# Two f32 halves for the second output piece of each group turn, and a later place for two low halves and six taps in VectorE's turn

## The chip, the cores and the metric
One core of a Trainium2 chip runs the whole program. The metric is the device time of the program in microseconds (us). There is no other core and no collective.

## The reference, cut to what matters
The reference is two model blocks in float32 on 256 tokens of width 1024. The first block computes `proj = rms_norm(x) @ w_in`. One part of it goes through a gated 31-tap depthwise convolution and a layer norm (the convolution branch), one through a grouped state-space branch of 8 groups, and the rest becomes gates. What the change touches is the end of the state-space branch:

```
y = ssd_chunked(...)                       # 8 groups, 256 channels each
y = y * silu(z)
yg = y.reshape(bsz, seqlen, N_GROUPS, D_INNER // N_GROUPS)
yg = yg * rsqrt(mean(yg * yg, axis=-1) + RMS_EPS)
y = yg.reshape(...) * norm_g
return y @ out_w                           # 2048 x 1024
```

Then come `w_out`, a feed-forward part, and a second block with its own projections. All of these are products of 256 tokens with large weight matrices that are read from HBM once.

## The kernel before, in words
All weights come as one stream of pieces, each 128 x 1024 f32 (512 KB), through a ring of 8 slots `raw`. SyncE starts the load of piece p when slot p % 8 is free, strictly in order of p (L415 to L427). Activations lie transposed, with channels on the 128 partitions and the 256 tokens on the free axis.

A piece is multiplied in one of two ways. In the usual way ScalarE copies it into `w_hi`, rounded to the TensorE format fp32r (L965), VectorE forms `w_lo` = `raw` - `w_hi` (L1457, "the low half"), and TensorE runs three matmuls for each 128 x 128 tile: hi x lo, hi x hi, lo x hi (`tile`, L485 to L490). The operand has such halves as well. In the native way a piece of the set `NATIVE` is multiplied in plain f32 straight from `raw` (L731 for the output pieces); the profile has two matmul records for each such matmul. Pieces of the set `LOW` get their low half in a third way: ScalarE writes minus `w_hi` into `w_lo` (L974), and a DMA issued by GpSimd adds `raw` to it (L462). The slot of a native piece is free when TensorE has used it, that of a usual piece when its low half is made, that of a `LOW` piece when its DMA has landed.

The eight groups run as a software pipeline. Group 0 has its own first turn. A hardware loop runs the turns of groups 1 to 6, and group 7 has a last turn with another mix of work (`more=False` in VectorE's `group_turn`). A turn of the loop takes eight pieces: six input pieces, at offsets 0, 1, 3, 4, 5, 7, and two output pieces of the group before, at offsets 2 and 6, both native. Between the pieces TensorE does small steps of the group: `cb` (L693), `x_transposes` (L701), `y_products` (L710), `y_transposes` in the middle of the second output piece (L718), and at the end `y_scale` (L611), which needs the scale that GpSimd forms from the group norm's mean square ("the moment").

The order of work on each engine is written out by hand. The names that matter:

- TensorE: `group_turn` at L738, `out_piece` at L725. The last turn follows the loop at L753 to L766. It goes on with input pieces of the gates, and at L762 to L766 it waits for `conv_sum_ready`, the sum over channels of the convolution, to compute its mean (L765).
- ScalarE: `group_turn` at L1099. It makes the high halves six pieces ahead, `silu_bc` (L1061) and `silu_x` (L1066) once VectorE has made the short convolution, `decays` (the exponential at L1081), the squares of y with their row sums (L1087), and drains of the input pieces from PSUM. The last turn stands at L1162 to L1189.
- VectorE: `group_turn` at L1724. The short convolution `conv_inputs` (L1658, twelve instructions), the taps of the 31-tap convolution (L1493, or `late_taps`, L1720, in the last turn), `masked_scores` (L1671, waits for `cb`), `x_by_dt` (L1676), `decayed_scores` (L1683, waits for `decays`, and TensorE's `y_products` waits for it), `y_gated` (L1692, L1696), the moment `y_mean` (L1467), `y_normed` (L1709), and between them one low half at each call of `lo()`. In the last turn the low halves and late taps are followed by six more taps (L1813), one low half (L1815), the channel sum (L1823), and the memset that signals `conv_sum_ready` (L1827).

Low halves in VectorE's loop turn, by offset from the turn's first piece: 8 after the short convolution, 11 after `y_gated`, 13 before `y_normed`. Offsets 7, 9 and 12 are `LOW`, so their call of `lo()` does nothing. In the last turn none but 1 and 4 is `LOW`, and VectorE makes 7 and 8 before `masked_scores`, 9 and 10 before the moment, 11, 12, 13 and 14 behind it.

Of the kernel before, what the change touches and what calls it, by code (L numbers as in the profile page):

```python
# [21 lines left out]
P = 128  # L22
# [53 lines left out]
DOWN2 = UP2 + 2 * KF2  # L76
PIECES = DOWN2 + KF2
GLU_NATIVE = (0, 1, 2, 3, 9)
NATIVE = frozenset(GLU_NATIVE) | frozenset([LOOP0 + 8 * i + n for i in range(GROUPS - 1) for n in OUT_AT]) | frozenset(range(TAIL0, PW0))
# [51 lines left out]

def split_order(p, turn=0):

    return sum(q not in NATIVE and q not in LOW for q in range(p)) + 1 + (6 - len(LOW_AT) if p < GATES0 else 8) * turn


def low_turn(p):
# [29 lines left out]
def hybrid_kernel(nc, x_in, weights, params_in, w_dt, lru_w, consts, out):  # L167
    cs_dram = nc.dram_tensor("cs_dram", [HEADS + HPG, T], F32).ap()
    stack = ExitStack()
    with stack:  # L170
# [22 lines left out]
        s0a = ExitStack()  # L193
        m_stage = sb("m_stage", [P, 2 * T], F32R, s0a)
        s0a.close()
        stage = sb("stage", [P, 2, T])
        stage2 = sb("stage2", [P, 2, T])
        sp = sb("sp", [P, 8, KD])
# [163 lines left out]
        cb_ready, cb_used, xt_ready, xdt_ready = sem("cb_ready"), sem("cb_used"), sem("xt_ready"), sem("xdt_ready")  # L362
        dec_ready, m_ready, y_ready, yz_ready = sem("dec_ready"), sem("m_ready"), sem("y_ready"), sem("yz_ready")
        yt_ready, first_tap = sem("yt_ready"), sem("first_tap")
        conv_operand_ready, mixed_ready = sem("conv_operand_ready"), sem("mixed_ready")
        m_copied = sem("m_copied")
        conv_high, conv_low = sem("conv_high"), sem("conv_low")
# [114 lines left out]
        def _(pe):  # L482
# [239 lines left out]
            def y_scale(g):  # L722
                spread_scale(g + 2)

            def out_piece(p, turn, g, c, between=None):  # L725
                native_loaded(p, turn)
                pe.wait_ge(scale_read, g + 2)
                for m in range(KD):
                    if between is not None and m == KD // 2:
                        y_transposes(between)  # L730
                    ins = mm(acc_out(m), raw[:, p % RING, m * P:(m + 1) * P], yn[:, c, :], start=False, stop=False,  # L731
                             skip_group_check=True)
                ins.then_inc(pieces_done, 1)
# [217 lines left out]
        def _(act):  # L951
# [131 lines left out]
            def y_squares(g):  # L1083
# [3 lines left out]
                    ins = F(ysq[:, t, :], A[3][:, t * T:(t + 1) * T], ACT.Square, accum_out=ysum[:, t:t + 1])  # L1087
                ins.then_inc(sums_ready, 1)

            for s in range(6):  # L1090
                split_hi(SSM0 + s + LEAD)
                drain_input(s, s, SSM0 + s, 0)
                if s == 2:
                    act.wait_ge(scale_read, 1)
                    exponents(0)
                if s == 3:
                    first_taps(0)

            def group_turn(g, base, t):  # L1099

                def split(n):
                    split_hi(base + n + LEAD, t)

                split(1)
                split(2)
                silu_bc(g)
                drain_input(0, 0, base + IN_AT[0], t)
                split(3)
                drain_input(1, 1, base + IN_AT[1], t)
# [50 lines left out]


            g = GROUPS - 1  # L1162
            for n in range(3):
                split_hi(GATES0 + n + LEAD)
            silu_bc(g)

            def conv_operand(c):

# [275 lines left out]
        def _(dve):  # L1444
# [256 lines left out]
            def y_normed(g, read=None):  # L1701
# [9 lines left out]
                        own.up(ins)  # L1711
                ins.then_inc(scale_read, 1)

            def late_taps(cs, ks=LATE_TAPS):

                last = {c: own.value() for c in cs}
                for k in ks:
                    for c in cs:
                        after(last[c])
                        last[c] = own.up(V.scalar_tensor_tensor(acc[:, c, :], v[:, c, k:k + T],  # L1720
                                                                col("conv_dw_w", c * CONV_K + k), acc[:, c, :],
                                                                ALU.mult, ALU.add))

            def group_turn(g, los, read=None, turn=0, more=True, first=True):  # L1724
# [7 lines left out]

                if first:
                    conv_inputs(g, (0, 1))
                    lo()
                    conv_inputs(g, (2, 3))
                lo()
                looped = more and first
                if looped:
                    taps(g + 1, LONG_TAPS[:2], start="sum")  # L1740
                masked_scores(g)
                turn_taps = LONG_TAPS[2:] if looped else LOOP_TAPS
                if not first:
                    lo()
                    more_taps(0, LOOP_TAPS[12:])
                    add_parts(0)
                    after(own.value())
                if looped:
                    more_taps(g + 1, turn_taps[:6])
                elif more:  # L1750
                    taps(g + 1, turn_taps[:6], start="sum")
                else:
                    late_taps((0, 1))
                x_by_dt(g)
                decayed_scores(g)
                lo()
                if more:
                    more_taps(g + 1, turn_taps[6:12])
                else:
                    late_taps((2, 3))  # L1760
                y_gated(g)
                lo(1 if first else 2)
                if more:
                    more_taps(g + 1, turn_taps[12:18])
                else:
                    late_taps((4, 5))
                if looped:
                    lo()
                    y_mean(g)
                else:  # L1770
                    y_mean(g)
                    lo()
                if more:
                    more_taps(g + 1, turn_taps[18:])
                    add_parts(g + 1)
                else:
# [620 lines left out]
```

## Time and profile before

| what | value |
|---|---|
| device time, median of 3 | 906.33 us (906.28 to 906.91) |
| the profiled execution | 907.11 us, span 905.0 us |
| TensorE (PE) busy | 895.5 us, 99% |
| VectorE (DVE) busy | 745.6 us, 82% |
| ScalarE (ACT) busy | 589.9 us, 65% |
| GpSimd (POOL) busy | 38.0 us, 4% |
| granted TensorE clock | 0.999 |

The difference of 2.1 us between the profiled execution's time and its span lies outside the instructions. Matmuls are pipelined: a matmul record of 0.28 us starts 0.12 us behind the one before it, so distances between starts are the cost, and not durations. The same holds in small for VectorE and ScalarE, where the next instruction often starts 0.1 us before the end that is shown.

### The profile page before, as it was taken

The page shows a single profiled execution, that of the slowest core. Times are in us where ns is not written, and L with a number is a line of the kernel's source. Part 1 is how long each engine was busy: PE and PEld are TensorE (multiplying, and loading weights), DVE is VectorE, ACT ScalarE, POOL GpSimd, SP SyncE. Part 2 cuts the span into 40 slices and gives each one's busy share as a digit, 9 for nine tenths or more (in the row PEclk, how much of TensorE's full clock was granted, in tenths as well). Part 3 has the DMA queues.
Part 4 walks back from the last instruction along what each step waited for, and adds up shares of the span by engine and source line. Part 5 has one row for each costly group of instructions (what it writes and reads, how often), then busy time and mean ns, then how long its engine had stood idle before and what let it go on. Part 6 is the DMA issues. An engine that isn't in the chain of part 4 may idle for free.

```text
span 905.0 us, 18388 instructions
## 1 busy us (share of the span) xinstructions
PE 895.5 (99%) x6629; PEld 846.7 (94%) x6629; DVE 745.6 (82%) x1387; ACT 589.9 (65%) x1020; POOL 38.0 (4%) x50
## 2 busy tenths in 40 slices
PE   9999999999999999999999999999999999999997
PEld 7999999999999999998888889989999999999886
DVE  5999898889889988889988666889979988888543
ACT  5649878798777485666666636679656756666432
POOL 1000111111110000000000000100000000000000
PEclk9999999999999999999999999999999999999999
DMA  8576578878876647447655555355447465555601
GB/s 335 179 270 228 146 196 237 243 209 242 227 202 207 210 146 251 163 141 248 204 186 185 197 187 171 123 194 188 144 137 258 148 202 183 178 180 177 232 2 46
DMA packets 48511, 172.05 MB, mean 190 GB/s; under 512 B 5668, under 2 KB 6344, under 8 KB 48328
## 3 DMA queue, kind: packets, MB, share of 16 engines
q1 hardware_dynamic: 43488, 154.74, 51.2%
q0 software_dynamic: 2880, 10.49, 6.1%
q10 hardware_dynamic: 2088, 6.08, 1.8%
q8 instruction: 35, 0.57, 0.2%
q14 instruction: 20, 0.16, 0.1%
HBM read 159.72 MB, written 1.09 MB: 178 GB/s over the span
## 4 chain that ended last, share of the span: by engine, by line
PE 68%; issue 24%; DVE 6%; ACT 1%; DMA 1%; POOL 1%; SPq 0%; POOLq 0%; DVEq 0%
PE A L488 10%; PE A L489 10%; PE A L490 10%; PE B L731 6%; PE A L522 4%; PE B L522 3%; PE B L812 2%; PE B L488 2%; PE B L489 2%; PE B L490 2%; PE A L524 2%; DVE w_lo L1457 2%; PE B L524 2%; PE A L812 2%; PE A L501 1%
## 5 line engine op out<-in xcount | busy, mean ns | idle before, releaser
L1457 DVE TENSOR_TENSOR w_lo<-raw,w_hi 128x1024 fp32r<-128x1024 f32 x249 | 301.8, 1220 | 63.5 <-ACT w_hi L965 62.4
L965 ACT ACTIVATE w_hi<-raw 128x1024 fp32r<-128x1024 f32 x249 | 259.2, 1051 | 69.9 <-PE A L813 20.6
L488 PE MATMUL A<-h,w_hi 128*128 128x256 f32 x957 | 276.0, 288 | 0.2 <-DVE sc L2120 0.2
L490 PE MATMUL A<-h,w_lo 128*128 128x256 f32 x957 | 270.7, 283 | 0.0
L489 PE MATMUL A<-h,w_hi 128*128 128x256 f32 x957 | 270.6, 283 | 0.0
L488 PEld LDWEIGHTS A<-h,w_hi 128*128 128x128 f32 x957 | 183.4, 192 | 3.3 <-issue 2.6
L489 PEld LDWEIGHTS A<-h,w_hi 128*128 128x128 f32 x957 | 183.5, 192 | 0.3
L490 PEld LDWEIGHTS A<-h,w_lo 128*128 128x128 f32 x957 | 183.3, 192 | 0.0
L488 PE MATMUL B<-h,w_hi 128*128 128x256 f32 x352 | 100.1, 284 | 0.0
L489 PE MATMUL B<-h,w_hi 128*128 128x256 f32 x352 | 99.6, 283 | 0.0
L490 PE MATMUL B<-h,w_lo 128*128 128x256 f32 x352 | 99.6, 283 | 0.0
L1493 DVE SCALAR_TENSOR_TENSOR part<-v,par,part 128x256 f32<-128x256 f32 x178 | 73.6, 479 | 0.0
L488 PEld LDWEIGHTS B<-h,w_hi 128*128 128x128 f32 x352 | 67.5, 192 | 0.8 <-issue 0.8
L489 PEld LDWEIGHTS B<-h,w_hi 128*128 128x128 f32 x352 | 67.5, 192 | 0.0
L490 PEld LDWEIGHTS B<-h,w_lo 128*128 128x128 f32 x352 | 67.5, 192 | 0.0
L812 PE MATMUL B<-hid,w_hi 128*128 128x512 f32 x184 | 64.1, 392 | 0.0
L731 PE MATMUL B<-yn,raw 128*128 128x256 f32 x256 | 59.1, 379 | 0.0
L522 PE MATMUL A<-h,w_hi 128*128 128x512 f32 x160 | 56.8, 399 | 0.0
L731 PEld LDWEIGHTS B<-yn,raw 128*128 128x128 f32 x256 | 47.0, 190 | 5.5
L813 PE MATMUL B<-hid,w_lo 128*128 128x256 f32 x184 | 51.4, 280 | 0.0
L812 PE MATMUL A<-hid,w_hi 128*128 128x512 f32 x138 | 48.1, 392 | 0.0
L522 PE MATMUL B<-h,w_hi 128*128 128x512 f32 x128 | 45.4, 399 | 0.0
(345 smaller groups left out, 1655.9 us busy)
## 6 DMA issues: line engine op xcount, KB each, us to landing
raw<-in_weights_dram SPq DMA_DIRECT2D x289, 512.0 KB, 4.4
w_lo<-raw POOLq DMA_DIRECT2D x20, 512.0 KB, 4.8
csrow<-cs_dram ACTq DMA_DIRECT2D x9, 512.0 KB, 4.8
x<-in_x_dram SPq DMA_DIRECT2D x4, 256.0 KB, 4.5
bd<-in_lru_w_dram ACTq DMA_DIRECT2D x1, 1024.0 KB, 5.5
out_dram<-m_wide SPq DMA_DIRECT2D x3, 256.0 KB, 2.1
raw<-in_weights_dram SPq DMA_DIRECT2D x2, 256.0 KB, 4.9
par<-in_params_dram SPq DMA_DIRECT2D x1, 379.0 KB, 6.6
```

What stands on the lines that cost most here:

```text
L488: mm(dst, wh, lo, start=first, stop=False, skip_group_check=free)
L489: mm(dst, wh, hi, start=False, stop=False, skip_group_check=free)
L490: return mm(dst, wl, hi, start=False, stop=last, skip_group_check=free)
L501: ins = mm(dst, raw[:, p % RING, k * P:(k + 1) * P], operand[:, k, :], start=k == 0, stop=k == KD - 1)
L522: mm(bank, w_hi[:, p % RING, k * P:(k + 1) * P], h[:, k, :], start=k == 0, stop=False, skip_group_check=True)
L524: ins = mm(bank[:, 0:T], w_lo[:, p % RING, k * P:(k + 1) * P], h_hi[:, k, :], start=False, stop=k == KD - 1, skip_group_check=True)
L731: ins = mm(acc_out(m), raw[:, p % RING, m * P:(m + 1) * P], yn[:, c, :], start=False, stop=False, skip_group_check=True)
L812: mm(DOWN_BANKS[m], wh, hid[:, k, :], start=first, stop=False, skip_group_check=True)
L813: return mm(DOWN_BANKS[m][:, 0:T], w_lo[:, slot, j * P:(j + 1) * P], hid_hi[:, k, :], start=False, stop=last, skip_group_check=True)
L965: F(w_hi[:, s, :], raw[:, s, :], ACT.Copy).then_inc(hi_ready, 1)
L1457: V.tensor_tensor(w_lo[:, s, :], raw[:, s, :], w_hi[:, s, :].bitcast(F32), ALU.subtract).then_inc(lo_ready, 1)
L1493: ins = V.scalar_tensor_tensor(dst, vs(k), w(k), dst, ALU.mult, ALU.add)
```

## The change: what it does
The second output piece of each turn (offset 6), for seven turns, leaves the set `NATIVE`. It is multiplied with `tile`, from `w_hi` and `w_lo`, with halves of the operand `yn` for its channel block: ScalarE makes `yn_hi` (`y_high`), VectorE `yn_lo` (`y_low`), in two new tiles. ScalarE's `split(0)` at the turn's start makes the piece's high half, and VectorE its low half. The slot of the piece is then free at its low half instead of at the end of its product.

In VectorE's loop turn the low halves are now 6 and 8 before the moment and 11 and 13 behind it (13 behind `y_normed`), and the taps 2 + 12 before it and 10 behind (before: 2 + 18 and 4). In the last turn it makes 6, 7 and 8 between `decayed_scores` and the moment, 9 and 10 right behind the moment, and 11, 12 and 13 behind `y_normed`. ScalarE's last turn gets the high half of piece 6 ahead of `silu_bc`, and those of 7 and 8 and `y_high` behind it.

```
-NATIVE = ... | frozenset([LOOP0 + 8 * i + n for i in range(GROUPS - 1) for n in OUT_AT]) | ...
+NATIVE = ... | frozenset([LOOP0 + 8 * i + OUT_AT[0] for i in range(GROUPS - 1)]) | ...
-    return ... + (6 - len(LOW_AT) if p < GATES0 else 8) * turn
+    return ... + (7 - len(LOW_AT) if p < GATES0 else 8) * turn
...
             def out_piece(p, turn, g, c, between=None):
-                native_loaded(p, turn)
-                pe.wait_ge(scale_read, g + 2)
+                split = p not in NATIVE
+                if split:
+                    split_ready(p, turn)
+                    pe.wait_ge(yn_low, g + 1)
+                else:
+                    native_loaded(p, turn)
+                    pe.wait_ge(scale_read, g + 2)
...
+                    if split:
+                        ins = tile(p % RING, m, yn_hi[:, c, :], yn_lo[:, c, :], acc_out(m), False, False, True)
+                        continue
...
+            def y_high(g, cs=(1,)):
+                act.wait_ge(scale_read, g + 2)
+                for c in cs:
+                    ins = F(yn_hi[:, c, :], yn[:, c, :], ACT.Copy)
+                ins.then_inc(yn_high, 1)
...
+                split(0)
                 split(1)
                 split(2)
                 silu_bc(g)
+                y_high(g - 1)
...
-            for n in range(3):
-                split_hi(GATES0 + n + LEAD)
+            split_hi(GATES0 + LEAD)
             silu_bc(g)
+            split_hi(GATES0 + 1 + LEAD)
+            y_high(g - 1)
+            split_hi(GATES0 + 2 + LEAD)
...
+            def y_low(g, cs=(1,)):
+                dve.wait_ge(yn_high, g + 1)
+                for c in cs:
+                    ins = V.tensor_tensor(yn_lo[:, c, :], yn[:, c, :], yn_hi[:, c, :].bitcast(F32), ALU.subtract)
+                ins.then_inc(yn_low, 1)
...
                 if first:
                     conv_inputs(g, (0, 1))
+                    conv_inputs(g, (2, 3))
+                else:
                     lo()
-                    conv_inputs(g, (2, 3))
-                lo()
...
+                cut = (4, 8, 12) if looped else (6, 12, 18)
...
                 decayed_scores(g)
                 lo()
+                if first:
+                    y_low(g - 1)
                 if more:
-                    more_taps(g + 1, turn_taps[6:12])
+                    more_taps(g + 1, turn_taps[cut[0]:cut[1]])
...
                 y_gated(g)
-                lo(1 if first else 2)
+                lo(2)
...
-                if looped:
-                    lo()
-                    y_mean(g)
-                else:
-                    y_mean(g)
-                    lo()
+                y_mean(g)
+                lo(2 if first else 1)
                 if more:
-                    more_taps(g + 1, turn_taps[18:])
+                    more_taps(g + 1, turn_taps[cut[2]:])
                     add_parts(g + 1)
                 else:
                     late_taps((6, 7))
-                lo()
+                if not first:
+                    lo()
                 y_normed(g, read)
                 lo(len(los))
```

## Rows read from the trace of the kernel before

**Rows 1.** The page: busy time, share of the span and instructions of each engine.
```profile
PE 895.5 (99%) x6629; PEld 846.7 (94%) x6629; DVE 745.6 (82%) x1387; ACT 589.9 (65%) x1020; POOL 38.0 (4%) x50
```

**Rows 2.** Waits of PE, 85 to 345 us: who waited for whom, in total, times, longest.
```profile
PE A L611 <- POOL scale L450: 0.5, 1, 0.5
```

**Rows 3.** Timeline of PE, turn of 134.41 us: start, length, engine, line, what.
```profile
147.22 0.60 PE L701 MATMUL A<-cst,gb 128*128 128x128 f32 x4
147.58 0.36 PE L488 MATMUL A<-h,w_hi 128*128 128x256 f32 x1
147.78 0.28 PE L489 MATMUL A<-h,w_hi 128*128 128x256 f32 x1
...
154.99 0.28 PE L490 MATMUL A<-h,w_lo 128*128 128x256 f32 x1
155.11 1.89 PE L731 MATMUL B<-yn,raw 128*128 128x256 f32 x8
...
158.82 0.47 PE L488 MATMUL A<-h,w_hi 128*128 128x256 f32 x1
159.12 0.28 PE L489 MATMUL A<-h,w_hi 128*128 128x256 f32 x1
```

**Rows 4.** Timeline of DVE in loop turns: convolution, a low half and what follows.
```profile
163.33 4.84 DVE L1658 SCALAR_TENSOR_TENSOR gb<-ubuf,par,gb 128x256 f32<-128x256 f32 x12
...
182.19 1.22 DVE L1457 TENSOR_TENSOR w_lo<-raw,w_hi 128x1024 fp32r<-128x1024 f32 x1
183.33 2.46 DVE L1493 SCALAR_TENSOR_TENSOR part<-v,par,part 128x256 f32<-128x256 f32 x6
...
204.08 1.76 DVE L1683 TENSOR_TENSOR dec<-dec,cbm 128x1536 f32<-128x1536 f32 x1
```

**Rows 5.** Timeline of ACT in loop turns: squares, exponential, a copy behind its load.
```profile
130.91 0.36 ACT L1087 ACTIVATE ysq<-A 128x256 f32<-128x256 f32 x1
...
147.29 1.49 ACT L1081 ACTIVATE dec<-dec 128x1536 f32<-128x1536 f32 x1
...
181.46 1.06 ACT L972 ACTIVATE w_hi<-raw 128x1024 fp32r<-128x1024 f32 x1 [2.39 <-DMA raw<-in_weights_dram]
...
212.74 0.38 ACT L1087 ACTIVATE ysq<-A 128x256 f32<-128x256 f32 x1
```

**Rows 6.** Timeline of PE: turn starts (L488), and the y products (L710).
```profile
189.60 0.36 PE L488 MATMUL A<-h,w_hi 128*128 128x256 f32 x1
...
205.90 0.66 PE L710 MATMUL A<-dec,xdt 128*64 128x256 f32 x4
...
217.27 0.36 PE L488 MATMUL A<-h,w_hi 128*128 128x256 f32 x1
...
272.46 0.36 PE L488 MATMUL A<-h,w_hi 128*128 128x256 f32 x1
```

**Rows 7.** The chain that ended last, in the last turn: start, length, what.
```profile
282.60 0.56 DVE cbm L1671
...
298.92 1.60 POOL scale L450
```

**Rows 8.** Timeline of DVE in the last turn and behind it.
```profile
277.65 1.23 DVE L1457 TENSOR_TENSOR w_lo<-raw,w_hi 128x1024 fp32r<-128x1024 f32 x1 [1.10 <-ACT w_hi L965]
...
311.91 0.27 DVE L1827 MEMSET part<- 128x256 f32 x1 [0.19 <-DVE sq_sum L1823]
```

**Rows 9.** Timeline of PE: the matmuls that wait for the memset's signal.
```profile
312.35 1.08 PE L765 MATMUL A<-sq_sum,cst 128*128 128x256 f32 x4
```

**Rows 10.** Timeline of ACT in the last turn: from L1061 to the exponential.
```profile
278.46 0.71 ACT L1061 ACTIVATE gb<-gb 128x256 f32<-128x256 f32 x2
...
283.01 1.49 ACT L1081 ACTIVATE dec<-dec 128x1536 f32<-128x1536 f32 x1
```

**Rows 11.** Timelines of ACT and DVE: a high and a low half of 256 tokens.
```profile
328.12 0.42 ACT L1172 ACTIVATE conv_hi<-acc 128x256 fp32r<-128x256 f32 x1
...
328.57 0.43 DVE L1845 TENSOR_TENSOR conv_lo<-acc,conv_hi 128x256 fp32r<-128x256 f32 x1
```

More of the change, by code:

```diff
@@ L78 @@
 GLU_NATIVE = (0, 1, 2, 3, 9)
-NATIVE = frozenset(GLU_NATIVE) | frozenset([LOOP0 + 8 * i + n for i in range(GROUPS - 1) for n in OUT_AT]) | frozenset(range(TAIL0, PW0))
+NATIVE = frozenset(GLU_NATIVE) | frozenset([LOOP0 + 8 * i + OUT_AT[0] for i in range(GROUPS - 1)]) | frozenset(range(TAIL0, PW0))
 LOW_AT = (1, 4, 7)
@@ L132, in split_order @@
 def split_order(p, turn=0):
-    return sum(q not in NATIVE and q not in LOW for q in range(p)) + 1 + (6 - len(LOW_AT) if p < GATES0 else 8) * turn
+    return sum(q not in NATIVE and q not in LOW for q in range(p)) + 1 + (7 - len(LOW_AT) if p < GATES0 else 8) * turn
 def low_turn(p):
@@ L195, in hybrid_kernel @@
         s0a.close()
+        s0 = ExitStack()
+        yn_hi = sb("yn_hi", [P, 2, T], F32R, s0)
+        yn_lo = sb("yn_lo", [P, 2, T], F32R, s0)
+        s0.close()
         stage = sb("stage", [P, 2, T])
@@ L364, in hybrid_kernel @@
         yt_ready, first_tap = sem("yt_ready"), sem("first_tap")
+        yn_high, yn_low = sem("yn_high"), sem("yn_low")
         conv_operand_ready, mixed_ready = sem("conv_operand_ready"), sem("mixed_ready")
@@ L723, in y_scale, with split_ready @@
                 spread_scale(g + 2)
-            def out_piece(p, turn, g, c, between=None):
-                native_loaded(p, turn)
-                pe.wait_ge(scale_read, g + 2)
+            def split_ready(p, turn):
+                if p in LOW:
+                    pe.wait_ge(low_added[(p - LOOP0) % RING], 16 * low_turn(p) + 16 * turn)
+                else:
+                    pe.wait_ge(lo_ready, split_order(p, turn))
+            def out_piece(p, turn, g, c, between=None):
+                split = p not in NATIVE
[5 more added lines that the diff above has]
+                    pe.wait_ge(scale_read, g + 2)
                 for m in range(KD):
@@ L1734, in group_turn @@
                     conv_inputs(g, (0, 1))
-                    lo()
-                    conv_inputs(g, (2, 3))
-                lo()
+                    conv_inputs(g, (2, 3))
+                else:
+                    lo()
                 looped = more and first
@@ L1748, in group_turn @@
                 if looped:
-                    more_taps(g + 1, turn_taps[:6])
+                    more_taps(g + 1, turn_taps[:cut[0]])
                 elif more:
@@ L1761, in group_turn @@
                 y_gated(g)
-                lo(1 if first else 2)
+                lo(2)
                 if more:
-                    more_taps(g + 1, turn_taps[12:18])
+                    more_taps(g + 1, turn_taps[cut[1]:cut[2]])
                 else:
                     late_taps((4, 5))
-                if looped:
-                    lo()
-                    y_mean(g)
-                else:
-                    y_mean(g)
-                    lo()
+                y_mean(g)
+                lo(2 if first else 1)
                 if more:
-                    more_taps(g + 1, turn_taps[18:])
+                    more_taps(g + 1, turn_taps[cut[2]:])
                     add_parts(g + 1)
```

## The prediction
> **What bounds the kernel now.** I read the page first, then who TensorE waits for in the stretch of the group turns, then its timeline there, then the same turns on VectorE and ScalarE, and last the chain that ended last. TensorE is busy 99%, VectorE 82%, ScalarE 65% [rows 1]. Between 85 and 345 us TensorE waits once, 0.5 us, for the scale of the last turn [rows 2]. So in the six loop turns (27.6 us each: 189.60 to 217.27 is 27.67 [rows 6]) it is the bound and every tenth taken from it would count, provided that nobody else comes late.
>
> Two places are nearly late already. The first is inside the loop turn: `y_products` starts 1.82 us behind the start of `decayed_scores` in the turn of 189.60 (204.08 [rows 4], 205.90 [rows 6]), because it waits for it. That is 16.30 us into the turn, where the other turns have 16.21; so the slack there is nothing. The second is the last turn. There the chain that ended last leaves TensorE at 282.60 and runs on VectorE to the moment and GpSimd at 298.92 [rows 7]. Behind it the memset that signals `conv_sum_ready` starts at 311.91 [rows 8] and the matmul that waits for it at 312.35 [rows 9], 0.44 us later, with no gap that shows as a wait. VectorE thus sets TensorE's time, or all but sets it, from 282.6 to 312.
>
> **TensorE's saving.** A usual tile's three matmuls start 0.12 us apart (154.99 to 155.11). Now the second output piece with the transposes in it takes from 155.11 to the next piece's second matmul at 159.12, 4.01 us. With halves it is 24 starts of 0.12 us, plus the transposes: 0.36 us from 147.22 to 147.58, then 0.20 instead of 0.12 us to 147.78, and 0.12 us to the next piece's second matmul: 2.87 + 0.36 + 0.08 + 0.12 = 3.43 us [rows 3]. That is -0.58 us a turn, -4.06 us for seven, if everything is in time. About 0.30 of the 0.58 lies in the piece's first half, ahead of the transposes.
>
> The trace prices the native piece at 3.71 us less its transposes, and the same piece in halves at 2.87. The Trainium skill (FP8 and Floating Point Precision, TensorE Precision Notes) has true f32 take four passes through the array. Against three passes that would be 4/3 of 2.87, or 3.83 us, and a saving of nearly 1 us a piece instead of 0.58; it would be 6.7 us in all, an estimate from that page's pass count. The rows decide, and they say less.
>
> **VectorE's and ScalarE's added work.** A turn gains one high half on ScalarE (1.06 us long [rows 5], 0.95 as a distance) and `y_high` (0.42, distance about 0.32 [rows 11]), and on VectorE one low half (182.19 to 183.33, 1.14 us [rows 4]) and `y_low` (0.43, distance 0.34 [rows 11]). As sums these fit. VectorE at 82% has some 3 us idle in a turn of 27.6, and needs 1.5. No DMA is added; the piece's slot comes free at its low half, some 17 us into the turn instead of 24.4, so loads start earlier if at all. The wait of `out_piece` for `yn_low` is met about 3 us ahead, and `yn_low` itself waits for `y_high`, ready 8 us ahead.
>
> **Where it doesn't fit: the ring through the loop.** Follow ScalarE around. From the squares of y (130.91) to the next turn's exponential (147.29) it is busy nearly without a gap: 16.38 us; the exponential is 1.49 us long [rows 5]. Then `decayed_scores` to `y_products` is 1.82 us, and from `y_products` to the squares of the same turn 205.90 to 212.74 is 6.84 us [rows 5, 6]. Around: 16.38 + 1.53 + 1.82 + 6.84 = 26.57 us, under the turn's 27.6. The change puts the high half and `y_high` ahead of the exponential, +1.27, and takes 0.30 from the last leg: 27.54 us. That is above the 27.02 that TensorE alone would need. So the turn takes about 27.5 us, and TensorE waits some 0.5 us at `y_products`.
>
> It starts worse. In turn 1 the squares are late already (130.91 is 24.1 us into the turn, against 23.1 in the turn of 189.60 [rows 5]), so turn 2's `y_products` comes at 130.91 + 16.38 + 1.27 + 1.53 + 1.82 = 151.9. Four rings on it is at 262.1 in turn 6. From there to the last turn's start is 217.27 - 205.90 = 11.37 [rows 6] less 0.58: 272.9, against 272.46 before. What ends a wait of ScalarE in the middle of the turn is a load (2.39 us at 181.46 [rows 5]). The added traffic is none, so its landing can help or hurt: if turn 1's squares come as early as TensorE allows, 1.35 us are given back. Ends for the start of the last turn are 269.0 (no ring, six times 0.58 saved) and 273.5; I take 272.2. The loop gives next to nothing.
>
> **The last turn.** Here VectorE's list decides. It starts late from the loop, as low halves 11 and 13 and ten taps now lie behind the moment instead of one half and four taps: 1.14 + 6 x 0.40 = 3.5 us more. That is caught up before `masked_scores`: the halves 7 and 8 no longer stand ahead of it, nor the wait of 1.10 us [rows 8], so it still starts when `cb` is ready, 282.60 - 272.46 = 10.14 us into the turn [rows 6, 7]. From there to the memset VectorE now has nine low halves instead of six and `y_low`: 3 x 1.14 + 0.34 = +3.76 us. ScalarE adds to it. The short convolution comes about 1 us later (it takes 4.84 us [rows 4], and the first half of it releases `silu_bc`, which began at 278.46), and between `silu_bc` and the exponential, 4.55 us apart now [rows 10], there will be two high halves and `y_high`, +2.2 us. The exponential then ends near 287.6 and `decayed_scores`, due at 286.9, waits 0.7 us. Bounds of that wait: 0 and 1.4; I take 0.7.
>
> So the memset comes 4.5 us later in the turn, and L765 with it, since the two have no slack [rows 8, 9]. TensorE's own 0.58 us and its old wait of 0.5 us go under in this: it will wait about 3 us at `y_scale` of the last turn and 2 us at L765. Behind L765 VectorE leads (mean, centring, squares, norm) and TensorE follows; I see no slack that takes anything back, and TensorE waits for nothing up to 345 us.
>
> **Sum.** 272.2 - 272.46 = -0.3 from the loop, +4.5 from the last turn: +4.2 us. The profiled execution, 907.11 us, would be 911.3; it stands 0.78 above the median of the runs, 906.33, and on that the forecast is 910.5 us.
>
> **Rivals.**
> - *Everything is covered.* The memset of the last turn is not what releases L765, VectorE's 18% of idle time takes the new work, and TensorE keeps all 4.06 us: 902.3 us. For it: TensorE's 99%, and the memset that ends before TensorE arrives. Against: the chain runs on VectorE for 16 us in just that turn. It decides if the memset starts earlier than 38.4 us into the last turn; before it was 39.45, and it has 3.8 us more to follow.
> - *No ring.* The loop keeps its 0.58 us a turn because loads land earlier and ScalarE starts its tail sooner. Then the last turn starts at 269.0, and VectorE and ScalarE come to it with less lead (the wait for the exponential is about 1.4): -3.5 + 3.76 + 1.4 = +1.7, 908.0 us.
> - *Half a ring.* A mixture, with half of the loop's saving kept and no wait for the exponential: -1.8 + 3.8 = +2.0 down to about +0.5 if the memset had slack of its own: 907.5 us.
> - *Worse.* Each landing that comes later than 19.2 us into a turn moves the ring on by what it is late, and nothing wins it back: up to +6, 912.3 us.
>
> **How the numbers follow.** Forecast 0.60, covered 0.13, no ring 0.10, half a ring 0.10, worse 0.07. About 0.2% (1.8 us) is what a measurement of this kernel can tell from no change. The forecast's own range is 909.0 to 911.6. The range given leaves out the covered case and most of the worse one: 906.2 to 912.2. Slower by over 0.2%: forecast and worse, half of no ring, and a little of half a ring, less a little for the forecast's lower end: 0.70. Same: 0.18. Faster: 0.12.
>
> **What would show it.** Each step has its mark in the profile after: 24 matmuls of L488 to L490's kind in the second output piece and 3.4 us for it; `y_products` 16.6 us or more into turns 3 to 6, released by `decayed_scores`, itself released by the exponential; turns 27.5 us long and the last one starting near 272; `masked_scores` of the last turn still released by `cb`; TensorE waiting about 3 us for the scale in the last turn and some 2 us for the memset at L765's place. I am wrong in the ring if turns are 27.0 us long, and wrong in the last turn if TensorE shows no wait there.

## The result, and the profile after

The changed kernel takes 910.57 us (median of 5 runs, 910.16 to 911.56) beside 906.91 us for the kernel before in the same session: a ratio of 1.0041 with a 95% interval of 1.0030 to 1.0052. It is slower, by 3.7 us. The forecast was 910.5. Only executions of one state are compared here; one of e2's eleven, at 1762.18 us, is outside it and left out. The profiled execution has a span of 908.6 us instead of 905.0. (In the kernel after, line numbers behind L193 are higher: `tile` is L493 to L495, `y_products` L715, the scale's transposes L616, the mean's matmul L785.)

The busy times hardly tell it. TensorE is busy 3.4 us less, VectorE 8.9 us more, ScalarE 8.4 us more, and TensorE's share falls from 99% [rows 1] to 98%. The first line of the page:

```profile
PE 892.1 (98%) x6685; PEld 845.2 (93%) x6685; DVE 754.5 (83%) x1401; ACT 598.3 (66%) x1034; POOL 43.2 (5%) x50
```

Who TensorE waited for from 85 to 350 us (total us, times, longest) tells it at once. Before there was a single row of 0.5 us [rows 2]:

```profile
PE A L616 <- POOL scale L455: 3.4, 1, 3.4
PE A L715 <- DVE dec L1714: 3.2, 6, 1.0
PE A L785 <- DVE part L1865: 0.9, 1, 0.9
```

Together 7.5 us of waits: 3.2 us at `y_products` in the turns, 3.4 us for the scale of the last turn, 0.9 us for the memset's signal. Less 0.5 that was there before, that is 7.0 us lost, against 4.3 us saved in seven pieces of 0.62 us; 2.7 us. The span grew by 3.6 us. Some 0.5 of the other 0.9 us lie at the same places, where the distances between starts grew by more than this view counts as waits: `y_products` comes 3.6 us later in the six turns together, where it counts 3.2, and the mean's matmul 1.10 us later than the matmuls ahead of it allow, where it counts 0.95. The rest isn't assigned to a place.

TensorE's timeline in the turn that starts at 189.54 (before: 189.60), columns start, length, engine, line, what: the piece in halves takes from 210.74 to 214.13, the next piece's second matmul, 3.39 us. Before it was 4.01 [rows 3]. `y_products` is 16.71 us into the turn, and its row names what it waited for.

```profile
189.54 0.36 PE L493 MATMUL A<-h,w_hi 128*128 128x256 f32 x1
...
206.25 0.66 PE L715 MATMUL A<-dec,xdt 128*64 128x256 f32 x4 [0.43 <-DVE dec L1714]
...
210.74 0.28 PE L493 MATMUL B<-yn_lo,w_hi 128*128 128x256 f32 x1
...
212.15 0.60 PE L723 MATMUL A<-cst,y 128*128 128x128 f32 x4
212.51 0.36 PE L493 MATMUL B<-yn_lo,w_hi 128*128 128x256 f32 x1
...
214.13 0.28 PE L494 MATMUL A<-h,w_hi 128*128 128x256 f32 x1
...
217.01 0.36 PE L493 MATMUL A<-h,w_hi 128*128 128x256 f32 x1
...
271.95 0.36 PE L493 MATMUL A<-h,w_hi 128*128 128x256 f32 x1
```

One step back in the same turn, first ScalarE's exponential, then VectorE's `decayed_scores`, which waits for it and starts 1.81 us before `y_products`:

```profile
202.92 1.49 ACT L1101 ACTIVATE dec<-dec 128x1536 f32<-128x1536 f32 x1
...
212.79 0.39 ACT L1107 ACTIVATE ysq<-A 128x256 f32<-128x256 f32 x1 [0.34 <-PE A L723]
```

```profile
204.44 1.76 DVE L1714 TENSOR_TENSOR dec<-dec,cbm 128x1536 f32<-128x1536 f32 x1 [0.54 <-ACT dec L1101]
```

The last turn on VectorE: `masked_scores` released by `cb` as before, `decayed_scores` by the exponential, then the moment 17.91 us behind `masked_scores` (before 16.1), then the memset.

```profile
282.08 0.56 DVE L1702 TENSOR_TENSOR cbm<-A,cst 128x384 f32<-128x384 f32 x1 [0.75 <-PE A L699]
...
286.73 1.76 DVE L1714 TENSOR_TENSOR dec<-dec,cbm 128x1536 f32<-128x1536 f32 x1 [0.25 <-ACT dec L1101]
...
299.99 0.16 DVE L1498 TENSOR_SCALAR moment<-ysum 128x2 f32<-128x2 f32 x1
...
315.48 0.27 DVE L1865 MEMSET part<- 128x256 f32 x1 [0.19 <-DVE sq_sum L1861]
```

And what waits for it on TensorE, the scale's transposes and the mean's matmul:

```profile
303.01 0.43 PE L616 MATMUL A<-cst,scale 128*128 128x128 f32 x2 [3.38 <-POOL scale L455]
...
315.90 1.10 PE L785 MATMUL A<-sq_sum,cst 128*128 128x256 f32 x4 [0.95 <-DVE part L1865]
```

The mean's matmul is at 315.90 instead of 312.35 [rows 9]: 3.55 us of the span's 3.6. Nothing is lost or won behind it.

A table of the places by which all runs below are read, from the timelines of the profiled executions, in us. "Turn 5 to 6" is the length of turn 5; `y_products` is its start, counted from the start of turn 5; "squares" and "moment" are counted from the start of turn 6, and the last three columns from the span's start.

| kernel | turn 5 to 6 | `y_products` | squares | moment | last turn starts | `masked_scores` there | mean's matmul |
|---|---|---|---|---|---|---|---|
| before | 27.60 | 16.22 | 23.80 | 24.65 | 272.46 | 282.60 | 312.35 |
| changed | 27.46 | 16.71 | 23.35 | 24.44 | 271.95 | 282.08 | 315.90 |
| e1 | 27.36 | 16.23 | 24.58 | 25.43 | 270.76 | 280.88 | 316.77 |
| e2 | 27.47 | 16.73 | 23.55 | 24.43 | 272.17 | 283.74 | 313.49 |
| e3 | 27.59 | 16.21 | 23.30 | 24.15 | 272.57 | 282.71 | 314.73 |
| e4 | 27.80 | 16.76 | 23.65 | 26.06 | 273.24 | 283.37 | 314.58 |
| e5a | 27.76 | 16.24 | 25.56 | 26.41 | 272.35 | 284.21 | 313.96 |
| e5b | 27.83 | 16.23 | 24.67 | 25.51 | 273.08 | 284.19 | 313.95 |
| e7 | 30.14 | 18.76 | 24.93 | 25.77 | 282.56 | 292.69 | 322.44 |
| e9 | 26.96 | 16.21 | 22.75 | 23.80 | 268.84 | 280.33 | 310.10 |
| e10 | 27.59 | 16.21 | 23.06 | 23.93 | 272.27 | 283.44 | 313.22 |
| e11 | 26.97 | 16.22 | 22.74 | 23.79 | 269.15 | 279.29 | 313.04 |
| e12 | 26.97 | 16.22 | 22.75 | 24.59 | 269.24 | 280.71 | 310.50 |
| e13 | 27.48 | 16.73 | 23.86 | 24.70 | 272.00 | 282.14 | 316.27 |

### The profile page after: what moved, and what is told of

Its sections match the earlier page's. It is cut to its first block, busy times and chain, and to the rows that moved or that the text cites. A ratio compares the mean times of both kernels' runs of the same rounds, so it can differ in the third digit from the quotient of the medians.

```text
span 908.6 us, 18547 instructions
## 1 busy us (share of the span) xinstructions
PE 892.1 (98%) x6685; PEld 845.2 (93%) x6685; DVE 754.5 (83%) x1401; ACT 598.3 (66%) x1034; POOL 43.2 (5%) x50
## 4 chain that ended last, share of the span: by engine, by line
PE 53%; issue 27%; DVE 9%; ACT 7%; DMA 2%; ACTq 1%; SPq 1%; POOL 0%; DVEq 0%; POOLq 0%
PE A L493 7%; PE A L494 7%; PE A L495 7%; PE A L527 4%; PE B L527 3%; DVE w_lo L1488 3%; PE B L493 2%; PE B L494 2%; PE B L495 2%; PE B L832 2%; PE A L529 2%; DMA raw<-in_weights_dram 2%; PE A L832 2%; PE B L529 2%; ACT dec L1096 2%
## 5 line engine op out<-in xcount | busy, mean ns | idle before, releaser
L1488 DVE TENSOR_TENSOR w_lo<-raw,w_hi 128x1024 fp32r<-128x1024 f32 x256 | 309.8, 1220 | 55.7 <-ACT w_hi L985 54.6
L985 ACT ACTIVATE w_hi<-raw 128x1024 fp32r<-128x1024 f32 x256 | 266.5, 1051 | 62.1 <-PE A L833 20.6
L493 PE MATMUL A<-h,w_hi 128*128 128x256 f32 x957 | 274.7, 287 | 0.2 <-DVE sc L2158 0.2
L495 PE MATMUL A<-h,w_lo 128*128 128x256 f32 x957 | 270.6, 283 | 0.0
L493 PEld LDWEIGHTS A<-h,w_hi 128*128 128x128 f32 x957 | 183.3, 192 | 3.1 <-issue 2.6
L495 PEld LDWEIGHTS A<-h,w_lo 128*128 128x128 f32 x957 | 183.3, 192 | 0.0
L493 PE MATMUL B<-h,w_hi 128*128 128x256 f32 x352 | 100.2, 285 | 0.0
L495 PE MATMUL B<-h,w_lo 128*128 128x256 f32 x352 | 99.6, 283 | 0.0
L493 PEld LDWEIGHTS B<-h,w_hi 128*128 128x128 f32 x352 | 67.3, 191 | 0.8 <-issue 0.8
L495 PEld LDWEIGHTS B<-h,w_lo 128*128 128x128 f32 x352 | 67.3, 191 | 0.0
L455 POOL TENSOR_TENSOR scale<-moment,half 128x2 f32<-128x2 f32 x16 | 22.5, 1407 | 659.4 <-DVE moment L1498 659.4
L529 PE MATMUL A<-h,w_lo 128*128 128x256 f32 x160 | 44.9, 281 | 0.0
```

The costliest lines, as they stand in the source:

```text
L455: nc.gpsimd.tensor_tensor(scale[:, :], moment[:, :], half[:, :], ALU.pow).then_inc(scale_ready, 1)
L493: mm(dst, wh, lo, start=first, stop=False, skip_group_check=free)
L495: return mm(dst, wl, hi, start=False, stop=last, skip_group_check=free)
L529: ins = mm(bank[:, 0:T], w_lo[:, p % RING, k * P:(k + 1) * P], h_hi[:, k, :], start=False, stop=k == KD - 1, skip_group_check=True)
L985: F(w_hi[:, s, :], raw[:, s, :], ACT.Copy).then_inc(hi_ready, 1)
L1488: V.tensor_tensor(w_lo[:, s, :], raw[:, s, :], w_hi[:, s, :].bitcast(F32), ALU.subtract).then_inc(lo_ready, 1)
```

## The experiments

The theory was the prediction's: a ring through ScalarE eats the loop's saving, and VectorE's longer list in the last turn sets the end. The rivals: that VectorE's order alone does it, that the halves alone do it, that ScalarE's idle time covers its work.

**e1: the exponential freed.** ScalarE's loop turn in the changed kernel:

```
-                split(0)
                 split(1)
-                split(2)
                 silu_bc(g)
-                y_high(g - 1)
...
                 decays(g)
+                split(0)
+                y_high(g - 1)
+                split(2)
```

> The changed kernel, but in ScalarE's loop turn the high halves of pieces 6 and 8 and the operand's high half stand behind the exponential instead of ahead of it. Ring theory: TensorE's wait for decayed_scores in the loop (3.2 us in six places in the changed kernel) goes, loop turns are 27.0 us long, the last turn starts at 269.0 instead of 271.95, its own length grows by about 0.25 us, and the time is 2.7 us under the changed kernel's 910.6: 907.9 us. Rival (the turn is held at 27.5 us by something else, the loads or VectorE's fuller list): turns stay 27.5 us long and the time stays within 0.5 us of 910.6.

Measured 909.9 us, 1.0037 of before (1.0023 to 1.0050). A miss of 2 us. The ring as such did break: `y_products` is back at 16.2 us into turns 2 to 6. But the turns are 27.0 to 27.7 us, not 27.0. On ScalarE the squares stand behind the copy of piece 12, and here that copy waits for its load (the row is 19.96 us into turn 5; in the changed kernel it is 17.93 in that turn, and 17.9 to 20.0 over the six):

```profile
235.64 1.06 ACT L992 ACTIVATE w_hi<-raw 128x1024 fp32r<-128x1024 f32 x1 [2.19 <-DMA raw<-in_weights_dram]
```

So the moment came later, at 25.43 us in turn 6, where VectorE waited 1.73 us for the squares, and took the ring's place: 268.47 us from the start, only 0.44 us earlier than in the changed kernel (268.91). The memset then came 0.44 us earlier too, 315.04 for 315.48. That is the second lesson of this run: the last turn doesn't hang on TensorE's start of it, but on that moment, through VectorE's list behind it, the short convolution and the exponential. A third effect spoils even the 0.44: after the wait of 3.39 us for the scale TensorE runs at half speed for some 5 us (granted clock 0.50 from 302 to 307 us), and the mean's matmul starts 1.73 us behind the memset instead of 0.42. The stretches 292 to 304 and 304 to 317 us (length, busy time and count of PE, PEld, DVE, ACT, POOL, then granted clock, DMA share, GB/s):

```profile
292.00:304.00 12.00, 8.52 (x66) 8.12 (x65) 11.96 (x24) 6.88 (x10) 2.73 (x1) 0.89 0.44 144
304.00:317.00 13.00, 13.00 (x95) 12.97 (x95) 12.81 (x24) 3.35 (x6) 0.00 (x0) 0.84 0.57 191
```

**e2: the last turn as before, the loop as changed.** `NATIVE` gets the last turn's second piece again, and both lists of the last turn are the old ones (their lines are left out here):

```
-... for i in range(GROUPS - 1)]) | frozenset(range(TAIL0, PW0))
+... for i in range(GROUPS - 2)] + [GATES0 + OUT_AT[0]]) | frozenset(range(TAIL0, PW0)) | frozenset([GATES0 + OUT_AT[1]])
```

> The changed kernel in the loop, but the last turn as before: its second output piece native, ScalarE's and VectorE's lists as before. Last-turn theory: VectorE comes to masked_scores about 1.5 us late (at 283.65 instead of 282.1), has 29.75 us to the matmul that waits for the memset, which is then at 313.4 instead of 315.9: 2.5 us under the changed kernel, 908.1 us. Rival (the last turn's extra VectorE work is not what costs; the loop alone does): 910.6 us, as the changed kernel.

907.88 us, 1.0012 (1.0002 to 1.0021). `masked_scores` at 283.74 and the mean's matmul at 313.49 are where they were expected, within 0.1 us. So 2.4 us (mean's matmul) to 2.7 us (medians) of the loss sit in the last turn's lists, and 1.1 us is what VectorE carries out of the loop: `masked_scores` comes 1.14 us later than before.

**e3: VectorE's order alone**, on the kernel before:

```
                 if first:
                     conv_inputs(g, (0, 1))
-                    lo()
                     conv_inputs(g, (2, 3))
-                lo()
+                else:
+                    lo()
...
+                cut = (4, 8, 12) if looped else (6, 12, 18)
```

and the calls behind it as in the change.

> The kernel before, with VectorE's new order alone: all output pieces native, no halves of the operand. Theory: the loop's turns stay at 27.6 us and the last one starts at 272.5; between masked_scores of the last turn and the memset VectorE has two low halves more (8 instead of 6), 2.28 us, so TensorE's matmul for the mean comes at 314.6 instead of 312.35 and the time is 2.3 us over before: 909.2 us. Rival (order is free, the halves cost all): 906.9 us. Second rival (the order makes the whole difference): 910.6 us.

910.16 us, 1.0038 (1.0024 to 1.0052); the profiled execution took 909.46. Its loop is that of before (27.6 us turns), and the mean's matmul is at 314.73, 2.4 us later, as expected. The median is 1.1 us above that. The profile of one execution can't show why; its four sister runs had lower mean clocks (0.997 and 0.998 beside 0.999) and took 0.3 to 1.0 us longer. Here TensorE waits 2.74 us for the scale, and in e1 and e13 the clock fell behind a wait of 3.39 and 2.45 us; in e3's own profiled execution it didn't (granted clock 1.00 from 302 to 312 us). That it is the cause here is argued, not shown.

**e4: the halves alone**, with VectorE's order of before (and `y_low` behind the low half that follows `decayed_scores`).

> The changed kernel with VectorE's order of before (18 taps ahead of the moment in the loop; low halves called for at the old places, so that in the last turn 6 and 7 stand ahead of masked_scores). Theory: the ring on ScalarE is as in the changed kernel, and the moment comes some 1.3 us later in the turn and begins to hold y_scale: turns of 27.5 to 27.7 us, last turn at 272.5; from masked_scores to the memset VectorE has one low half and the operand's low half more than before, 1.48 us: 1.0 to 1.5 us under the changed kernel, 909.3 us. Rival (the order is what pays for the halves, without it the moment is far too late): above 911.5 us.

909.18 us, 1.0024 (1.0014 to 1.0033). Turns 3 to 5 are 27.8 us, because the moment is now at 26.06 us and holds the scale, while `y_products` is late as in the changed kernel (16.76 us). That is as the theory said, though by a little more; the last turn starts at 273.24. There VectorE has 1.5 us more to do, and the mean's matmul is at 314.58. So the new order is worth having in the loop (it gives 1.3 us at the last turn's start) and costs more than it gives in the last turn.

**e7: ScalarE's load alone.** The kernel before, with two copies of 128 x 1024 into a tile that nobody reads, at the start of each loop turn:

```
+                for b in range(2):
+                    n = own.up(F(scratch[:, :], x[:, 0:4, :].rearrange("p a t -> p (a t)"), ACT.Copy))
+                    act.wait_ge(act_steps, n)
                 split(1)
```

> The kernel before, and nothing else changed but two further copies of 128 x 1024 on ScalarE at the start of each loop turn, ahead of the exponential, 2.2 us together, into a tile that nobody reads. Ring theory: the ring through ScalarE, decayed_scores, y_products and the squares is 26.57 + 2.2 = 28.8 us, so the turns 2 to 6 are near 28.8 us instead of 27.6, y_products waits in each, and the time is 5.5 to 7 us over before: 912 to 913.5 us. Rival (ScalarE at 65% has 5 us idle in a turn, which takes 2.2 us): 906.6 us.

916.26 us, 1.0101 (1.0085 to 1.0116), so 9.4 us slower, where 5.5 to 7 had been expected. From the squares to the next exponential it is now 18.6 us, 2.2 more than before. Turns 4 and 6 take 28.8 us, as computed for the ring; turns 2, 3 and 5 take 29.7 to 30.2. Turns 3 and 5 follow one in which the squares stood behind the landing of piece 12 (its copy starts 22.58 us into turn 2 and 21.61 into turn 4): in turn 4 it is 8.23 us from `y_products` to the squares, where it is 6.84 in turn 3. So a late load adds to the ring, and the 9.4 us are not the ring's alone. The waits are at `cb` as well as at `y_products`:

```profile
PE A L696 <- ACT gb L1064: 4.6, 5, 1.6
PE A L713 <- DVE dec L1689: 3.8, 6, 0.7
```

The turns of 28.8 us are 1.2 us longer than before, for 2.2 us of added work: what was taken up is the 1.0 us by which the ring was shorter than the turn, and ScalarE's 5 us of idle time took up nothing beyond that.

**e5a and e5b: e1 and e2 together, with fewer taps behind the moment.** `cut = (6, 10, 15)`. In e5a the seven taps left stand directly behind the moment, in e5b the low half 11 does. From e5b to e5a:

```
                 y_mean(g)
-                lo(2 if first and more else 1)
+                if not (first and more):
+                    lo()
                 if more:
                     more_taps(g + 1, turn_taps[cut[2]:])
                     add_parts(g + 1)
+                    if first:
+                        lo(2)
```

> Halves in the six loop turns only. ScalarE makes the high halves of 6 and 8 and of the operand behind the exponential; the last turn is as before the change (native, old lists); VectorE's loop turn has 2 + 15 taps ahead of the moment and 7 behind it, and directly behind the moment come taps, not a low half. Theory (the ring is broken, and what VectorE carries out of the loop is small): turns of 27.0 to 27.2 us, last turn starts at 269 to 270 (before: 272.46), masked_scores there about 1 us late, the matmul for the mean at 310.2 to 311 (before: 312.35), time 904.5 to 905.5 us, under both kernels. GpSimd's scale takes 0.96 us in the loop. Rival (landing of the loads or VectorE's moment takes the place of the ring as in the experiment before, where the last turn started at 270.8): 906.5 us or more.

> As the kernel with the taps first, but a low half directly behind the moment in VectorE's loop turn. Theory (GpSimd's scale takes 1.65 us instead of 0.96 when VectorE runs a 128 x 1024 subtraction beside it, as the runs so far show): the scale comes 0.7 us later, which where the moment is later than 24.3 us into the turn holds TensorE: turns 0.2 to 0.6 us longer, time 1 to 2.5 us over the kernel with the taps first. Rival (GpSimd's span is only a rough record, and its length holds nobody): the same time within 0.4 us.

909.2 us, 1.0025 (1.0015 to 1.0036), and 909.37 us, 1.0030 (1.0018 to 1.0041). Both miss: the rival of the first holds, that landings take the ring's place. The copy of piece 12 starts 21.5 us into turn 6 of e5a:

```profile
265.86 1.06 ACT L992 ACTIVATE w_hi<-raw 128x1024 fp32r<-128x1024 f32 x1 [2.71 <-DMA raw<-in_weights_dram]
```

and the moment is there 26.4 us into the turn, with VectorE idle for 2.3 us before it, waiting for the squares. GpSimd's scale did take 0.96 us in e5a and 1.65 us in e5b, but the moment came earlier in e5b, so that the price of the 0.7 us isn't measured by this pair.

**e9: the squares ahead of piece 12.** From e5a: ScalarE has, behind the exponential, pieces 6, 8, 9 and 11, then first taps and squares, and only then 12 and 13; GpSimd forms the scale before it adds piece 12. `cut = (6, 10, 14)`.

```
                 decays(g)
                 split(0)
                 y_high(g - 1)
                 drain_input(2, 2, base + IN_AT[2], t)
                 split(2)
                 split(3)
                 split(5)
...
                 y_squares(g)
                 drain_input(4, 4, base + IN_AT[4], t)
                 split(6)
                 split(7)
...
-                add_raw(LOOP0 + 8 * i + 12)
                 rsqrt(i + 3)
+                add_raw(LOOP0 + 8 * i + 12)
```

> Halves in the six loop turns, last turn as before. ScalarE's loop turn in a new order: ahead of the exponential only piece 7; behind it the high halves of 6, 8, 9, 11 and of the operand; then the first taps and the squares of y, and only behind them pieces 12 and 13, so that no load's landing stands ahead of the squares. GpSimd forms the scale ahead of its addition for piece 12. VectorE has 2 + 14 taps ahead of the moment, 8 behind it. Theory (in the runs with the exponential freed, the landing of piece 12, 20 to 21.5 us into a turn, took the ring's place and held squares, moment and scale): moment at 23.6 to 24.3 us, turns of 27.0 us, last turn starts at 268.9, matmul for the mean at 309.5 (before: 312.35), time 903.7 to 904.5 us. Rival (TensorE's or VectorE's list itself has no room for 27.0 us turns): 907 us or more.

904.47 us, 0.9970 of before (0.9959 to 0.9981): faster than both kernels, 2.3 us under the one before and, by the two differences from it, 6.0 us under the changed one. All six turns are 26.96 to 26.99 us, the moment is at 23.80 in each, and TensorE waits for nobody in the loop. The start of the last turn and the mean's matmul here (before: 272.46 and 312.35):

```profile
268.84 0.36 PE L493 MATMUL A<-h,w_hi 128*128 128x256 f32 x1
...
310.10 1.05 PE L785 MATMUL A<-sq_sum,cst 128*128 128x256 f32 x4
```

Of the 3.6 us saved in the loop 2.3 arrive. VectorE comes to `masked_scores` 1.35 us later in the last turn than before (11.49 us into it for 10.14), though it waits only 0.68 us for a high half from ScalarE on the way, where it waited 1.10 [rows 8]; the rest of its list is what it was.

**e10: the same orders without the halves.** All second pieces native again.

> The kernel with the squares ahead of piece 12's load, but with all output pieces native: same orders on ScalarE, GpSimd and VectorE, no halves of the second output pieces. Theory (the new orders alone gain nothing, since TensorE's turn of 27.6 us is then the bound): turns of 27.6 us, last turn at 272.5, 906.7 us as before, and the difference to the kernel with halves is the 6 x 0.58 us of TensorE. Rival (the reordering is what gains): as the kernel with halves.

908.14 us, 1.0013 (1.0004 to 1.0022). The turns are 27.59 us. The new orders alone don't gain; they cost 1.4 us by the medians and 0.87 us at the mean's matmul, since VectorE comes 1.0 us late to `masked_scores` of the last turn (11.17 us into it) and no saving pays for it. The expectation had left that out. Between e10 and e9 lie 3.7 us, for six pieces in halves: the turns differ by 0.62 us, and 6 x 0.62 is 3.7.

**e11: the changed kernel with ScalarE's and GpSimd's order of e9.** VectorE's lists and the last turn as changed.

> The changed kernel with ScalarE's and GpSimd's new loop order alone; VectorE's lists and the whole last turn as in the changed kernel. Theory: turns of 27.0 us, moment of the last loop turn at 266 instead of 268.9, and since the last turn hangs on that moment through low halves, ten taps, short convolution and exponential, the memset comes 2.5 to 3 us earlier than in the changed kernel: 907.7 us. Rival (the last turn's lists cost what the loop gains, whatever it starts from): 910 us or more.

907.76 us, 1.0009 (1.0000 to 1.0018). Turns of 26.97 us, and the mean's matmul at 313.04, 2.9 us before the changed kernel's. So the hold-ups in the loop cost the change 2.7 us (3.66 over before against 0.99; 2.8 by the medians alone): the ring and the landing behind it together, since e1, which removes the ring alone, brought the memset only 0.44 us forward. The two orders were moved together, so their shares aren't known.

**e12: two taps fewer behind the moment of e9.** `cut = (6, 11, 16)`.

> The fastest kernel so far (904.5 us) with two taps more ahead of the moment in VectorE's loop turn: 2 + 16 ahead, 6 behind. Theory (what VectorE carries out of the loop behind the last moment costs the last turn one to one; the moment has 1 us of slack in the loop): moment at 24.6 instead of 23.8 us into the turn, turns still 27.0 us. The last turn's masked_scores starts as before at 11.5 us into the turn, because VectorE arrives there at the same time (its whole list up to there is the same length), so the time stays 904.5 us within 0.3 us. Rival (two taps fewer behind the moment are 0.8 us earlier in the last turn): 903.7 us.

904.77 us, 0.9976 (0.9966 to 0.9986), the same as e9. The moment is 0.79 us later, and `masked_scores` of the last turn 11.47 us into it instead of 11.49. VectorE's one wait between the loop's last moment and there, for a high half from ScalarE, is 0.67 us here and 0.68 in e9, so it arrives at the same time: what counts is the sum of its list, not where the moment stands in it.

**e13: the last turn's taps ahead of its two low halves**, on the changed kernel.

> The changed kernel; in the last turn alone the eight taps that followed the low halves 9 and 10 stand ahead of them, directly behind the moment. Theory (GpSimd's scale is slowed by VectorE's subtractions beside it: 2.73 us behind two, 1.6 behind one, 0.96 behind taps): the scale takes 0.96 to 1.2 us, TensorE's wait for it falls from 3.4 to about 1.7 us, but the memset comes at the same time, so the wait for the memset grows from 0.9 to about 2.7 us and the time stays 910.4 us within 0.4 us. Rival (the wait for the scale is what costs): 1.5 us less, 909 us.

911.45 us, 1.0043 (1.0029 to 1.0057), with runs from 909.54 to 912.57. The waits moved as expected:

```profile
PE A L715 <- DVE dec L1714: 3.4, 6, 1.0
PE A L785 <- DVE part L1867: 2.5, 1, 2.5
PE A L616 <- POOL scale L455: 1.6, 1, 1.6
```

The wait for the scale fell by 1.8 us and the one for the memset grew by 1.6, and the mean's matmul is at 316.27, no earlier. So 3.4 us is the largest wait of the changed kernel and yet not what costs: who takes 1.8 us of it away gets 1.6 back at the next wait. In the profiled execution, one of the long ones, the clock fell behind that second wait (mean 0.83 from 312 to 322 us).

## Why the prediction was right

- *TensorE's saving*, 0.58 us a piece: the piece in halves took 3.39 us and not 3.43, so the saving is 0.62. The four passes that the Trainium skill gives for true f32 (FP8 and Floating Point Precision, TensorE Precision Notes) would have made it nearly 1 us, if every pass cost what an fp32r matmul costs. The trace does not agree with that estimate. Before, four native tiles take from 155.11 [rows 3] to 156.84, 0.43 us each, and three fp32r matmuls are 0.36 us: a ratio of 0.83 and not 3/4. The rows don't speak against the count of passes: a quarter of 0.43 is 0.108 us, while fp32r matmuls start 0.12 us apart. e9 and e10, 3.7 us apart for six pieces, bear the smaller saving out.

```profile
156.84 0.60 PE L718 MATMUL A<-cst,y 128*128 128x128 f32 x4
```

- *The ring*, 27.54 us: turns 4 to 6 are 27.46 to 27.48, `y_products` 16.7 us into them, released by `decayed_scores`, and that by the exponential. From the squares of turn 5 to the exponential of turn 6 it is 17.62 us, where 16.38 + 1.27 had been added up. e1 takes the added work off the ring and has `y_products` back at 16.2, e7 makes the ring longer by ScalarE alone and gets longer turns, and e11 has neither the ring nor the landing behind it and gets 26.97. Shown.
- *The start of the ring.* Turn 1's squares came at 23.31 us instead of 24.12, so 0.8 of the 1.35 us that I held possible were given back. The last turn started at 271.95, and 272.2 was taken.
- *The last turn.* Three low halves and `y_low` between `masked_scores` and the memset, 3.76 us: measured 315.48 - 282.08 = 33.40 against 311.91 - 282.60 = 29.31 [rows 7, 8], 4.09 us more, of which 0.25 is the wait for the exponential. That wait was the term sized wrongly: 0.7 was taken, within bounds of 0 and 1.4. The 2.2 us of added work between `silu_bc` and the exponential came (6.62 us apart instead of 4.55), but `silu_bc` began 0.13 us later than before and not about 1 us, so that the exponential ended near 286.7 instead of 287.6:

```profile
278.59 0.81 ACT L1081 ACTIVATE gb<-gb 128x256 f32<-128x256 f32 x2 [1.83 <-DVE gb L1689]
...
285.21 1.49 ACT L1101 ACTIVATE dec<-dec 128x1536 f32<-128x1536 f32 x1
```

- *The sum*: +4.2 was said, the mean's matmul moved by 3.55 and the span by 3.6. The forecast of 910.5 beside a measured 910.57 is closer than the working was, and that is luck: the change was put 0.5 us too high, and the kernel before was taken at 906.33, where it then measured 906.91, 0.58 higher.
- *The split of the waits*: 3 us for the scale and 2 for the memset were said, 3.4 and 0.9 measured. The second is under half of what was said. The first would have been some 1.1 us smaller if GpSimd's scale had taken 1.59 us as before; it took 2.73, which was not in the working. So that figure too is in part luck.
- *The rivals.* "Covered" is out by the waits. "No ring" was priced at +1.7 us; e11 is that case in the flesh, and measures +1.0 us beside its own runs of before (+0.85 beside 906.91). "Half a ring" did not occur.
- What I had not seen is what comes after the ring. I took it that without it the loop would run at 27.0 us. In e1 and e5a it didn't: the landing of piece 12 stood next in line, and only the order of e9, which moves that too, has 27.0 (e9, e11 and e12).

What stays open is what sets the landing of piece 12. Its copy starts 17.9 to 20.0 us into the turns of the changed kernel, 18.5 to 20.1 in the kernel before, 19.6 to 20.6 in e1 and 20.1 to 21.5 in e5a. No run separates the order of ScalarE's copies, GpSimd's additions and the loads themselves.

## What to carry to other kernels

Before work is put into the idle time of an engine, follow the ring once around: from an instruction of that engine, through everybody whom it makes wait, to the same instruction one turn later. If the ring is as long as the bound engine's turn, the idle time isn't free, whatever the share says (here 65% busy, and 1.3 us more work a turn, with the landing that stood next in line, kept 2.7 us of the saving from arriving). And look at the turn behind the loop by itself: what a moved step leaves over has to be paid where the lists end, and the largest wait there isn't always the one that costs.

## What the runs showed of the hardware

GpSimd's power of 128 x 2 elements takes 0.69 us where VectorE runs nothing beside it, 0.87 to 0.99 us when VectorE runs `SCALAR_TENSOR_TENSOR` taps beside it (0.87 in loop turns of e4, 0.91 in e13's last turn, 0.96 to 0.99 in the loop turns of the kernel before), 1.59 to 1.66 us when it runs one 128 x 1024 f32 subtraction, and 2.73 us beside two of them. The rows are the kernel before behind its group turns, e13's last turn, a loop turn of the changed kernel, and its last turn:

```profile
377.26 0.69 POOL L450 TENSOR_TENSOR scale<-moment,half 128x2 f32<-128x2 f32 x1 [52.99 <-DVE moment L1467]
```

```profile
300.53 0.91 POOL L455 TENSOR_TENSOR scale<-moment,half 128x2 f32<-128x2 f32 x1 [29.40 <-DVE moment L1498]
```

```profile
241.68 1.65 POOL L455 TENSOR_TENSOR scale<-moment,half 128x2 f32<-128x2 f32 x1 [3.44 <-DVE moment L1498]
...
300.23 2.73 POOL L455 TENSOR_TENSOR scale<-moment,half 128x2 f32<-128x2 f32 x1 [29.40 <-DVE moment L1498]
```

It looks as though GpSimd's power is finished only some 0.7 us after the VectorE instruction beside it has ended. A tap takes 0.40 us and a subtraction 1.14, start to start: in the changed kernel's last turn the two subtractions run from 300.06 to about 302.3, and the power ends at 302.96. The Trainium skill (VectorE: DVE Perf Modes, "Two Vector instructions with no wait between them") says that an instruction with two SBUF tensor inputs reads the second through an interface that is shared with GpSimd. The rows agree: taps and subtractions both have two such inputs, and both lengthen the power. Why it waits for two subtractions in a row, but through a row of eight taps for one at most, no run shows.

TensorE's granted clock fell after a wait in some executions and not in others: after 3.39 us in e1 (matmuls 0.21 us apart instead of 0.12 from 302.9 to 307.7 us, which is the 1.2 GHz level) and after 2.45 us in e13, but not after 3.38 us in the profiled execution of the changed kernel, nor after 3.41 us in e11. In e13 the run with a mean clock of 1.0 took 909.54 us, and those with 0.996 and 0.997 took 911.45 and 912.53; but two with 0.998 took 910.05 and 912.57, so the mean clock alone doesn't order the runs.
